# Cache pages loaded as 32 rows of 8 KB or as 128 rows of 2 KB, in a one-core decoder step

## The chip, the cores and the metric

The kernel runs on one core of a Trainium2 chip. The metric is the device time of one execution in microseconds (us). Its work is done by TensorE (matrix products), VectorE, ScalarE and GpSimd, and by 16 DMA engines that move data between DRAM and the on-chip memory of 128 partitions (SBUF). DMA instructions are issued by SyncE and GpSimd. In the profile TensorE is PE, VectorE DVE, ScalarE ACT, GpSimd POOL and SyncE SP.

## What is computed

One layer of a hybrid decoder for a prompt of 1024 tokens and for eight sample sequences of eight new tokens each. The part that the change touches is the attention of the samples over their cached past: 4096 tokens for each sequence, kept in pages of 128 tokens that a page table names. A token's row has 512 floats of keys (4 heads of 2 x 64) and 512 of values (4 heads of 128), 2 KB each.

```python
k_past = cache_k[i, page_table].reshape(DB, past_len, DIFF_HEADS, 2, DIFF_DH)
v_past = cache_v[i, page_table].reshape(DB, past_len, DIFF_HEADS, DIFF_DV)
...
s_past = jnp.einsum('bqhcd,bkhcd->bhcqk', q, k_past).astype(F32) * scale
a = jax.nn.softmax(jnp.concatenate([s_past, s_new], axis=-1), axis=-1)
w = (a[:, :, 0] - lam * a[:, :, 1]).astype(v.dtype)
return (jnp.einsum('bhqk,bkhv->bqhv', w[..., :P], v_past)
        + jnp.einsum('bhqk,bkhv->bqhv', w[..., P:], v))
```

All old tokens are visible to all new ones. With 8 sequences of 32 pages, 256 pages of keys and 256 of values are read, 256 KB each, 134 MB in all.

## The kernel before

The program runs its phases one after the other: input projection, gated linear attention, `attention`, and the dense stages (output projection, FFN, embedding). The phase `attention` interleaves two jobs. One is the causal attention of the prompt, in 32 units (4 heads by 8 query blocks). The other is the paged attention of the samples, in 64 groups of four pages (`NKV`), eight for each sequence.

TensorE, ScalarE and VectorE each follow an order written out by hand over `STEPS` = 74 steps. In step t, for t below 64, TensorE turns the keys of group t: four transposes of 128 x 128 for each of the four heads (line 1587), reading `m.kr[:, slot, p, ...]`, where p is the page in the group. ScalarE and VectorE copy them to `dec_kt`, and a step later the scores are formed (L1599). Nine steps behind (`LAG`), in step t, the group t - 9 has its exponentials transposed (L1622) and multiplied with its values (L1641), reading `m.vr[:, slot, p, ...]`. Transposes and products of the prompt lie in between (L1560, L1569, L1547). So steps 0 to 8 have keys alone, steps 9 to 63 keys and values, and steps 64 to 73 values alone.

`m.kr` (keys, tile `dec_k`) and `m.vr` (values, tile `dec_v`) are rings of four slots, of four pages each (`KR`, `VR` = 4): a slot is 128 partitions by 4 x 512 floats. `load_pages` (L1299) fills a slot with four DMAs, one for each page; the page number is read from the table into a register first. SyncE issues the key groups, in the gated-linear-attention phase the first three (`PRE`), and group n, from 4 on, after TensorE has turned the last head of group n - 4 (semaphore `ring_filled`, L1390). On its queue lie also the loads of the prompt's keys (L1309, 64 partitions each, lower and upper half in turn) and queries (L1316). GpSimd issues the value groups: the first four when TensorE has turned key groups 0, 2, 4 and 6, and group n when the values of group n - 4 have been used (`pv_done`, L1422). TensorE waits for the four DMAs of a group in `turn_keys` (L1581) and `values` (L1638).

Other transfers that are looked at below: the prompt and sample activations `x_in` at the start (L289: 128 partitions in rows of 4 KB; L294: 64 partitions), followed by weights in rows of 512 B, and `feat_swap` (L316), a copy inside SBUF from 32 partitions to 32 others in rows of 4368 B.

Of the kernel before, what the change touches and what calls it, by code (L numbers as in the profile page):

```python
# [829 lines left out]
def gla(nc, io, m, ps, scr, sems):  # L830
# [31 lines left out]
    with nc.Block() as block:  # L862

        @block.sync
        def _(sp):

            sp.dma_start(m.gvs[:, :], scr["gv_s"]).then_inc(s["v_loaded"], 16)
            sp.dma_start(m.gv[:, NC // 2:NC, :], scr["gv_p"].rearrange("(c p) f -> p c f", p=P)[:, NC // 2:NC]
                         ).then_inc(s["v_loaded"], 16)
            for pr in range(2):  # L870
                sp.dma_start(m.s0[:, pr], io["state_gla"][0, :, 2 * pr:2 * pr + 2].rearrange("b h k v -> (h k) b v")
                             ).then_inc(s["s_loaded"], 16)
            sp.wait_ge(table_in, 16)
            load_pages(sp, m.ids, io["cache_k"], m.kr, 0, pages_in[0], 0)
            for part in range(4):
                load_keys(sp, m, scr, 0, part, head_k_in)
            for n in range(2):
                load_queries(sp, m, scr, n, head_q_in[n])
            for n in range(1, PRE):
                load_pages(sp, m.ids, io["cache_k"], m.kr, n, pages_in[n], n)  # L880
            sp.wait_ge(s["kd_turned"], NC)
            sp.wait_ge(s["q1_ready"], 2 * NC)
            sp.wait_ge(s["qpe_ready"], 2)
            sp.wait_ge(s["s_kd"], 1)
            sp.dma_start(m.qs[:, :, :], scr["qS"].rearrange("h p t -> p h t")).then_inc(new_in, 16)
            sp.dma_start(m.kts[:, :, :], scr["kS"].rearrange("h p t -> p h t")).then_inc(new_in, 16)
            sp.dma_start(m.table[:, :], io["page_table"].rearrange("(o b) n -> o (b n)", o=1)).then_inc(ids_in, 16)
            sp.dma_start(m.lam[:, :, :], io["lam_params"].broadcast_to([P, 4, DK])).then_inc(lam_in, 16)
            sp.wait_ge(s["s_updated"], 2 * NC)
            for pr in range(2):  # L890
                sp.dma_start(io["new_gla_prompt"][2 * pr:2 * pr + 2].rearrange("h k v -> (h k) v"), m.s[:, pr]
                             ).then_inc(s["stored"], 16)
# [406 lines left out]
def load_pages(eng, ids, cache, ring, slot, sem, n):  # L1299

    for p in range(4):
        page = eng.value_load(ids[0:1, 4 * n + p:4 * n + p + 1], min_val=0, max_val=POOL - 1)
        eng.dma_start(ring[:, slot, p:p + 1, :], cache[bass.ds(page, 1)].rearrange("o t f -> t o f")).then_inc(sem, 16)  # L1303


def load_keys(eng, m, scr, h, part, sem):
# [12 lines left out]
def attention(nc, io, m, ps, scr, sems):  # L1319
# [57 lines left out]
    with nc.Block() as block:  # L1377

        @block.sync
        def _(sp):  # L1380
            sp.wait_ge(ids_in, 16)
            for n in range(PRE, KR):
                load_pages(sp, m.table, io["cache_k"], m.kr, n, k_page_in[n], n)
# [1763 lines left out]
```

## Time and profile before

| | |
|---|---|
| three runs, us | 1882.27, 1882.73, 1886.83 |
| median, us | 1882.73 |
| span of the profiled execution, us | 1880.3 |
| attention phase within the span | about 433 to 868 us |
| TensorE busy over the whole span | 1773.0 us (94%) |
| VectorE, ScalarE, GpSimd busy | 1192.5 (63%), 735.6 (39%), 341.2 us (18%) |
| bytes moved by DMA | 265.73 MB, mean 141 GB/s |

The profiled execution has a record of its span alone, from the first to the last instruction: 1880.3 us, 2.4 us below the median of the three runs. Times in rows are microseconds from the start of the span. A row with `x8` merges or groups eight instructions; `a<-b` means that tile a is written from tile b; L1587 is line 1587. The granted clock of TensorE (PEclk) is a share of full speed, and DMA share is the mean busy share of the 16 DMA engines; it can come out a little over 1.

### The profile page before, as it was taken

To read this page: it belongs to the slowest core of one execution; us is meant where nothing else is said; L and a number is where in the kernel's file an instruction comes from. 1 tells how busy PE (TensorE), PEld (TensorE's weight loads), DVE (VectorE), ACT (ScalarE), POOL (GpSimd) and SP (SyncE) were. 2 spreads that over 40 slices of the span, in tenths; PEclk is the share of its full clock that TensorE was granted. 3 is DMA by queue.
4 is the path that set the end of the run, shared out by engine and by line. 5 is a ranking of instruction groups with operands and counts; after the bars stand their busy time and mean duration, and the time that the engine had idled before them with its cause. 6 is when DMAs were issued, how large, how long until landed. Compare 5 with 4: busy or idle time off the path is not lost.

```text
span 1880.3 us, 35481 instructions
## 1 busy us (share of the span) xinstructions
PE 1773.0 (94%) x13062; PEld 1639.1 (87%) x13062; DVE 1192.5 (63%) x1946; ACT 735.6 (39%) x1418; POOL 341.2 (18%) x360
## 2 busy tenths in 40 slices
PE   6999999996999999996999999999999999999998
PEld 6999999984666667665998999999999999999997
DVE  4223742475777777765458876667677878699443
ACT  5113322564655565653225333222323424245320
POOL 1111331001233333332111211211121000000110
PEclk9999999898999999998999999999999999999998
DMA  5323551227999999977111222222222424232121
GB/s 162 108 80 82 141 140 56 61 83 236 330 350 354 346 357 360 353 231 226 35 45 46 80 69 81 81 70 69 81 70 69 157 81 134 74 106 86 47 69 48
DMA packets 232923, 265.73 MB, mean 141 GB/s; under 512 B 16162, under 2 KB 173428, under 8 KB 232756
## 3 DMA queue, kind: packets, MB, share of 16 engines
q1 hardware_dynamic: 211988, 195.36, 33.2%
q0 software_dynamic: 20768, 68.17, 10.7%
q8 instruction: 101, 1.65, 0.4%
q14 instruction: 66, 0.54, 0.1%
HBM read 229.79 MB, written 29.21 MB: 138 GB/s over the span
## 4 chain that ended last, share of the span: by engine, by line
PE 45%; DVE 6%; ACT 1%; issue 1%; DMA 1%; POOL 0%; DVEq 0%; ACTq 0%
PE psum L2518 33%; PE psum L150 10%; DVE x_second_lo L2532 1%; DVE unit_lo L1910 1%; DMA x_first_hi_raw<-scratch_z 1%; PE psum L2197 0%; PE psum L2894 0%; DVE x_second_lo_raw L2536 0%; DVE rstd_and_products L2576 0%; DVE x_first_lo L2532 0%; DVE h L2576 0%; ACT unit_hi L1904 0%; DVE rstd_and_products L2009 0%; DVE x_lo L2226 0%; DMA w_raw<-in_w_ple_gate 0%
## 5 line engine op out<-in xcount | busy, mean ns | idle before, releaser
L2518 PE MATMUL psum<-x_second_hi,unit_hi 128*128 128x364 f32 x924 | 304.5, 330 | 8.0 <-DVE x_second_lo L2532 4.6
L2518 PE MATMUL psum<-x_second_hi,unit_lo 128*128 128x364 f32 x924 | 303.4, 328 | 0.0
L2518 PE MATMUL psum<-x_second_lo,unit_hi 128*128 128x364 f32 x924 | 303.4, 328 | 0.0
L1303 POOL DMA_DIRECT2D dec_v<-in_cache_v x256 | 137.6, 538 | 288.1 <-issue 282.2
L150 PE MATMUL psum<-x_hi,w_hi 128*128 128x364 f32 x768 | 182.0, 345 | 5.8 <-DVE x_lo L2226 5.8
L2518 PEld LDWEIGHTS psum<-x_second_hi,unit_hi 128*128 128x128 f32 x924 | 173.8, 188 | 10.8 <-issue 5.7
L2518 PE MATMUL psum<-x_first_hi,unit_hi 128*128 128x364 f32 x528 | 173.7, 329 | 0.6 <-DVE x_first_lo L2532 0.6
L2518 PEld LDWEIGHTS psum<-x_second_hi,unit_lo 128*128 128x128 f32 x924 | 174.0, 188 | 0.0
L2518 PEld LDWEIGHTS psum<-x_second_lo,unit_hi 128*128 128x128 f32 x924 | 173.7, 188 | 0.0
L2518 PE MATMUL psum<-x_first_hi,unit_lo 128*128 128x364 f32 x528 | 173.5, 329 | 0.0
L2518 PE MATMUL psum<-x_first_lo,unit_hi 128*128 128x364 f32 x528 | 173.2, 328 | 0.0
L150 PE MATMUL psum<-x_hi,w_lo 128*128 128x364 f32 x768 | 170.2, 330 | 0.0
L150 PE MATMUL psum<-x_lo,w_hi 128*128 128x364 f32 x768 | 169.8, 329 | 0.0
L1470 ACT ACTIVATE dec_kt<-psum 128x512 f32<-128x512 f32 x192 | 108.6, 599 | 154.6 <-PE psum L1587 154.6
L1904 ACT ACTIVATE unit_hi<-unit_sums 128x512 fp32r<-128x512 f32 (+1 forms) x136 | 83.3, 618 | 217.2 <-PE psum L2518 184.7
L1587 PE MATMUL psum<-consts,dec_k 128*128 128x128 f32 x1024 | 139.3, 281 | 20.2 <-DMA dec_k<-in_cache_k 8.8
L2397 POOL TENSOR_TENSOR w_raw<-w_raw,gains 128x1024 f32<-128x1024 f32 x42 | 88.7, 2111 | 379.6 <-DMA w_raw<-in_w_ffn_gate 210.8
L1904 ACT ACTIVATE unit_hi<-w_raw 128x512 fp32r<-128x512 f32 (+1 forms) x136 | 82.5, 617 | 178.2 <-PE psum L2518 155.8
L1587 PEld LDWEIGHTS psum<-consts,dec_k 128*128 128x128 f32 x1024 | 115.2, 143 | 39.2 <-issue 15.7
L150 PEld LDWEIGHTS psum<-x_hi,w_hi 128*128 128x128 f32 x768 | 131.5, 189 | 15.2 <-DVE x_lo L2226 6.2
L150 PEld LDWEIGHTS psum<-x_lo,w_hi 128*128 128x128 f32 x768 | 133.9, 189 | 0.0
L150 PEld LDWEIGHTS psum<-x_hi,w_lo 128*128 128x128 f32 x768 | 133.8, 189 | 0.0
(313 smaller groups left out, 3313.3 us busy)
## 6 DMA issues: line engine op xcount, KB each, us to landing
dec_k<-in_cache_k SPq DMA_DIRECT2D x256, 256.0 KB, 5.7
dec_v<-in_cache_v POOLq DMA_DIRECT2D x256, 256.0 KB, 5.5
w_raw<-in_w_in SPq DMA_DIRECT2D x25, 512.0 KB, 3.9
scratch_z<-ffn_hidden SPq DMA_DIRECT2D x22, 546.0 KB, 2.8
w_raw<-in_w_ffn_gate SPq DMA_DIRECT2D x22, 512.0 KB, 3.8
w_raw<-in_w_ffn_up SPq DMA_DIRECT2D x22, 512.0 KB, 3.8
w_raw<-in_w_ffn_down SPq DMA_DIRECT2D x16, 512.0 KB, 4.0
feat_swap<-feat_n SPq DMA_DIRECT2D x32, 136.5 KB, 2.4
```

What stands on the lines that cost most here:

```text
L150: ins = pe.matmul(out[:, c, 0:SPAN], w(k), x(k)[:, c * SPAN:c * SPAN + SPAN], start=n == 0 and w is whi and x is xhi, stop=n == len(ks) - ...
L1303: eng.dma_start(ring[:, slot, p:p + 1, :], cache[bass.ds(page, 1)].rearrange("o t f -> t o f")).then_inc(sem, 16)
L1470: act.activation(m.kt[:, t % 2, h, :], ring_bank(("keys", t, h)), ACT.Copy).then_inc(d["ring_act"], 1)
L1587: ins = pe.transpose(ring_bank(key)[:, p * P:p * P + P], m.kr[:, t % KR, p, h * P:h * P + P], ident)
L1904: act.activation(m.uhi[unit][:, 0:half_tiles(t), :], unit_source(m, t, unit), ACT.Copy).then_inc(s["w_hi"], 1)
L1910: dve.tensor_tensor(m.ulo[unit][:, 0:n, :], unit_source(m, t, unit), f32(m.uhi[unit][:, 0:n, :]), ALU.subtract).then_inc(s["w_lo"], 1)
L2397: gp.tensor_tensor(m.raw[:, u], m.raw[:, u], gain(m, "ffn").unsqueeze(2).broadcast_to([P, KT, P]), ALU.mult).then_inc(s["w_scaled"], 1)
L2518: ins = pe.matmul(bank[b], w[unit][:, j, :], x[slot][:, j, :], start=start and j == 0 and w is m.uhi and x is m.xhi7, stop=j == k - 1 and ...
L2532: dve.tensor_tensor(m.xlo7[slot][:, 0:n, :], source, f32(m.xhi7[slot][:, 0:n, :]), ALU.subtract).then_inc(s["x_lo"], 1)
```

## The change

Each of the four DMAs of a group still moves one page of 256 KB to the same slot. Before, the page's 128 tokens went to 128 partitions, 2 KB each, in column block p of the slot. After, the page goes to 32 partitions, 32p to 32p+31: partition 32p + t receives the four neighbouring tokens 4t to 4t+3, side by side in the four column blocks, one row of 8 KB in DRAM and in SBUF. A column block of the slot then holds 32 tokens of each of the four pages. The change applies to keys and values alike.

```diff
     for p in range(4):
         page = eng.value_load(ids[0:1, 4 * n + p:4 * n + p + 1], min_val=0, max_val=POOL - 1)
-        eng.dma_start(ring[:, slot, p:p + 1, :], cache[bass.ds(page, 1)].rearrange("o t f -> t o f")).then_inc(sem, 16)
+        eng.dma_start(ring[32 * p:32 * p + 32, slot, :, :].rearrange("t j f -> t (j f)"),
+                      cache[bass.ds(page, 1)].rearrange("o (t j) f -> (o t) (j f)", j=4)).then_inc(sem, 16)
```

## Rows read from the trace of the kernel before

**Rows 1.** Busy time by stretch: us and (instructions) of each engine, clock, DMA share, GB/s.

```profile
core 0: us, PE busy (x) PEld busy (x) DVE busy (x) ACT busy (x) POOL busy (x), PEclk, DMA share, GB/s
433.00:494.00 61.00, 45.12 (x333) 30.46 (x337) 37.52 (x83) 29.16 (x70) 10.55 (x18) 0.88 0.98 316
494.00:828.00 334.00, 314.95 (x3937) 234.94 (x3927) 247.96 (x523) 200.51 (x513) 114.63 (x214) 1.00 1.00 342
828.00:868.00 40.00, 27.11 (x422) 19.15 (x420) 19.41 (x38) 12.37 (x37) 18.29 (x29) 0.86 0.69 211
500.00:800.00 300.00, 281.31 (x3510) 209.10 (x3502) 223.10 (x473) 180.11 (x462) 102.94 (x192) 1.00 1.02 352
```

**Rows 2.** TensorE's waits from 425 to 870 us: total us, times, longest us.

```profile
PE psum L1587 <- DMA dec_k<-in_cache_k: 8.8, 1, 8.8
...
PE psum L1641 <- DMA dec_v<-in_cache_v: 4.5, 2, 2.4
```

**Rows 3.** Waits of SyncE, which issues the key loads, from 433 to 868 us.

```profile
SPq L1302 <- PE psum L1587: 51.1, 30, 4.2
```

**Rows 4.** TensorE in order of time: start us, us, line, what it writes and reads.

```profile
494.05 1.06 PE L1641 MATMUL psum<-dec_v,dec_pt 128*32 128x128 f32 x32
...
826.73 1.04 PE L1587 MATMUL psum<-consts,dec_k 128*128 128x128 f32 x8
...
830.30 1.06 PE L1641 MATMUL psum<-dec_v,dec_pt 128*32 128x128 f32 x32
```

**Rows 5.** DMA queues from 500 to 800 us: packets, MB, share of 16 engines.

```profile
q1 hardware_dynamic: 32183, 54.64, 53.0%
q0 software_dynamic: 15349, 50.29, 48.3%
```

**Rows 6.** DMA from 3 to 14 us: all packets, then the queue of SyncE.

```profile
DMA packets 1297, 4.53 MB, mean 412 GB/s; under 512 B 208, under 2 KB 208, under 8 KB 1297
...
q1 hardware_dynamic: 1297, 4.53, 102.8%
```

**Rows 7.** DMA from 157 to 162 us; last line: issues, KB each, us to landing.

```profile
DMA packets 192, 0.56 MB, mean 112 GB/s; under 512 B 64, under 2 KB 64, under 8 KB 192
...
q1 hardware_dynamic: 192, 0.56, 50.3%
...
feat_swap<-feat_n SPq DMA_DIRECT2D x4, 136.5 KB, 2.4
```

**Rows 8.** DMA from 377.0 to 378.6 us, the same columns.

```profile
DMA packets 260, 0.44 MB, mean 278 GB/s; under 512 B 43, under 2 KB 43, under 8 KB 260
...
q1 hardware_dynamic: 260, 0.44, 84.7%
...
att_k<-scratch_kT SPq DMA_DIRECT2D x2, 128.0 KB, 3.2
```

**Rows 9.** DMA from 14.7 to 15.7 us, and from 16.2 to 17.6 us.

```profile
DMA packets 204, 0.19 MB, mean 186 GB/s; under 512 B 15, under 2 KB 179, under 8 KB 204
...
DMA packets 807, 0.41 MB, mean 290 GB/s; under 512 B 15, under 2 KB 807, under 8 KB 807
```

**Rows 10.** SyncE's queue in order of time, one merged piece of eight key loads.

```profile
606.12 8.86 SPq L1303 DMA_DIRECT2D dec_k<-in_cache_k  x8
```

**Rows 11.** DMA of the opening stretch (433 to 494 us), and issues from 828 us.

```profile
DMA packets 9625, 19.25 MB, mean 316 GB/s; under 512 B 1192, under 2 KB 1892, under 8 KB 9618
...
dec_v<-in_cache_v POOLq DMA_DIRECT2D x27, 256.0 KB, 3.7
```

**Rows 12.** Issuing a DMA on SyncE: duration ns min/median/max, first and last start.

```profile
L1303 SPq DMA_DIRECT2D dec_k<-in_cache_k x256: 332/338/3964, 368.2 to 809.3; - x128
...
L316 SPq DMA_DIRECT2D feat_swap<-feat_n x32: 507/591/606, 157.0 to 260.4; - x32
```

**Rows 13.** Busy time by stretch, ahead of the phase; columns as in rows 1.

```profile
420.00:440.00 20.00, 14.39 (x135) 12.22 (x133) 12.43 (x30) 10.33 (x35) 1.97 (x2) 0.83 0.28 92
```


## The prediction

> **What bounds the kernel now.** I first asked for the busy times of the engines in four stretches, because the change only touches the attention phase, which lies between 433 and 868 us [rows 1]. In the long middle stretch TensorE is busy 315 of 334 us at full granted clock, so at first sight it sets the pace. The column to look at beside it is the DMA share: 1.00, and 1.02 between 500 and 800 us. The 16 DMA engines are occupied all the time as well, and move 342 to 352 GB/s. Two resources are full at once, and the next question is who waits for whom.
>
> TensorE's own waits over the phase [rows 2] name a DMA in two rows only: 8.8 us once for a key page and 4.5 us in two pieces for value pages. The list of the DMA-issuing queue [rows 3] shows the reverse: SyncE waits 51 us in 30 pieces for TensorE to empty a slot of the key ring. So the loads run ahead of TensorE, by up to the four groups that each ring holds, and are throttled by it. TensorE bounds the phase and the DMA engines just keep up: anything that lowers their rate by more than a few per cent makes them the bound.
>
> The rhythm follows from TensorE's order of instructions [rows 4]. The value products of step 9 (the first ones) begin at 494.05 us, those of step 63 (the last step that also turns keys) at 830.30 us. That is 54 steps in 336.3 us, 6.23 us each. In each the DMA engines move 342 GB/s x 334 us / 53.6 steps = 2.13 MB: one group of four key pages, one of four value pages, and a few queries. The break-even rate is therefore 2.13 MB / 6.23 us = 342 GB/s.
>
> **The change part by part.** The number of DMA instructions (256 for keys, 256 for values), their bytes, their semaphores and their places in the queues stay the same. What changes is the shape: 32 rows of 8 KB to 32 partitions, where 128 rows of 2 KB went to 128. Inside a group, token 4t+j of a page now sits at partition t, block j, for keys and values alike. A softmax sum doesn't depend on the order of its terms and all old tokens are visible, so no instruction is added on any compute engine: 0 us there.
>
> *Packets.* Today 192 value loads leave 15349 packets on their queue [rows 5]: 192 x (64 + 16) = 15360, so two rows already share a packet of 4 KB, plus 16 completion packets. Larger packets help where the DMA is the bound. 4 KB rows to 128 partitions move 4.53 MB in 102.8% of 11 us, 400 GB/s of busy time [rows 6], against 345 GB/s (352 / 1.02) for the present mix. Were the destination as wide as now, the DMA would gain some slack, and TensorE would only lose its two DMA waits: at most 13 us.
>
> By the Trainium skill, DMA: Bandwidth & Descriptors, "Why small descriptors are slow", a packet costs about three fixed cycles beside one for every 32 bytes. An estimate from that page is 67 cycles for 2 KB and 259 for 8 KB, 3% less per byte; it speaks for the change, and no run here isolates it.
>
> *Destination.* What speaks against the change is the width. The trace has one transfer of the new width: `feat_swap`, four DMAs of 136.5 KB, each to 32 partitions in rows of 4368 B [rows 7]. They leave 64 small completion packets, 16 for each, so all 16 DMA engines take part. But 0.56 MB occupies them for 50.3% of 5 us: 222 GB/s, or 13.9 GB/s for an engine where the wide load got 25. It isn't a perfect twin (SBUF to SBUF), so I looked for loads from DRAM. The keys of the prompt go to 64 partitions, the upper and the lower half in turn, in rows of 2 KB [rows 8]: 0.44 MB in 84.7% of 1.6 us, 325 GB/s. At 14.7 us, where the 64-partition `x_in` sample is mixed with the weights queued behind it, the rate falls to 0.19 MB in 1 us, 186 GB/s, between 400 GB/s before [rows 6] and 290 GB/s after it, with the weights alone in rows of 512 B [rows 9]. I read these as: narrow transfers to the same half of the partitions slow each other to about half, those to different halves little.
>
> The Trainium skill states a reason in SBUF — State Buffer, "Door 1: The DMA port swizzle": partitions 0 to 31 reach 8 of 16 ports, with 218 GB/s as the asymptote and 189 GB/s at 1 MiB, and two loads to partitions 0 and 64 at once gained 6%. The 222 GB/s of [rows 7] agree with its asymptote, the 325 GB/s of [rows 8] with its 6% do not. By that page alone the whole phase would go at about 200 GB/s, which is an estimate; the rival below works such a case out from rows.
>
> In a group, pages 0 and 1 go to the lower half of the partitions and pages 2 and 3 to the upper. The key group is issued by SyncE after the step's transposes, the value group by GpSimd after the value products, and SyncE often issues two groups on end [rows 10]. Nothing ties a key page to a value page on the same half, so I take half of the bytes at 222 GB/s (same half) and half at 325 GB/s (other half): (4.50 + 3.08) / 2 = 3.79 us per MB, 264 GB/s. The bounds are 186 GB/s below [rows 9] and 400 GB/s above [rows 6]; I stay nearest to [rows 7], the only row of the same width.
>
> *The sum.* A step takes 2.13 x 3.79 = 8.07 us in place of 6.23: 54 x 1.84 = 99 us. The opening, 433 to 494 us, moves 19.25 MB [rows 11]: 73 us in place of 61, 12 us. In the tail, 828 to 868 us, only values are left: 27 value loads (7.1 MB) at 222 GB/s take 32 of its 40 us [rows 1, 11], so little is lost there: 2 us. Together 113 us. The span of 1880.3 us becomes 1993 us; the three runs have their median 2.4 us above that span, so the forecast is 1996 us.
>
> *Costs taken as nothing.* SyncE needs 338 ns to issue a key load and 591 ns for a 32-partition `feat_swap` [rows 7, 12]. Four times 0.25 us is 1 us a step on a queue that waited about 1 us a step for TensorE [rows 3]; uncovered it would be a few us in all, and in a step of 8.07 us it is covered. GpSimd's issue lies on an engine with nothing else to do. TensorE's 315 us in 334 become about 5.9 us of work in a step of 8.07 us, 73% busy; where it was busy 72% (14.39 of 20 us) its granted clock was 0.83 on average, between its two levels of 1.2 and 2.4 GHz [rows 13]. At 0.83 the 5.9 us become 7.1 us and stay hidden behind the DMA. At the lower level throughout they would not, but then TensorE would again be busy all the time.
>
> **The rivals.** *Half rate throughout* (chance 0.28). The DMA engines work through key and value pages in step, so that they meet on the same half whichever page is up. For it: [rows 7, 9]. Against it: [rows 8]. At 222 GB/s a step takes 9.60 us, 54 x 3.37 = 182 us, the opening 26 us more, the tail 3: 211 us, 2094 us. At the 186 GB/s of [rows 9] it is 282 + 42 + 6 = 330 us, 2213 us.
>
> *No difference* (0.11). Key and value pages lie on different halves most of the time, or the slow `feat_swap` belongs to SBUF as a source and not to the destination; then the rate stays at or over the 342 GB/s of the break-even and TensorE goes on setting the step. For it: the 325 GB/s of [rows 8] are close to it already. The change would also do nothing if 8 KB rows were cut into packets of today's size and the width didn't matter. 1883 us.
>
> *Faster* (0.11). As before, but the larger rows lift the rate towards the 400 GB/s of [rows 6] and the key wait of 8.8 us at the opening and the value waits of 4.5 us in the tail go away: 1883 - 13 = 1870 us. It decides itself at a sustained rate over 342 GB/s in the middle stretch; under that it can't be.
>
> **How the numbers follow.** The forecast, a phase bound by the DMA with halves partly shared, has 0.50 (some 1890 to 2060 us). Two runs of this kernel differ by up to 0.3%, which is about what can be told from no change. The first two cases are slower: 0.78; no difference 0.11; faster 0.11. The range reaches from 1878 us, which takes in the case of no difference, to 2150 us, which takes in the half-rate case down to about 205 GB/s; left out are the faster case and some 0.07 above.
>
> **What would show it right or wrong.** Right: in the changed profile the value products of steps 9 and 63 lie about 436 us apart, DMA share stays near 1.00 while the rate drops to about 264 GB/s, TensorE waits some 100 us for key or value pages inside the middle stretch, SyncE's waits for TensorE remain but the loads land later, and value loads leave 32 + 16 packets each. The granted clock in the middle stretch falls under 1.00. The time after the phase is unchanged. Wrong: a rate of 342 GB/s or more at the new width (the width doesn't bind), or about 222 or less with the step at 9.6 us (no sharing of halves at all), or TensorE's work itself longer.

## The result and the profile after

The changed kernel takes 2053.25 us (median; 2046.95 to 2057.34), the one before 1884.78 us in the same runs. The ratio is 1.0893, with a 95% interval from 1.0874 to 1.0912: some 168 us slower. The span of the profiled execution grew from 1880.3 to 2051.7 us, by 171.4 us.

Nearly all of it lies in the attention phase, which now reaches to about 1040 us (868 before); what follows takes 1012 us in both. The busy times by stretch answer to [rows 1] (us and instructions of each engine, granted clock, DMA share, GB/s):

```profile
core 0: us, PE busy (x) PEld busy (x) DVE busy (x) ACT busy (x) POOL busy (x), PEclk, DMA share, GB/s
433.00:494.00 61.00, 37.96 (x245) 26.13 (x245) 27.89 (x65) 21.05 (x49) 9.87 (x18) 0.79 1.00 238
494.00:1000.00 506.00, 368.00 (x4065) 280.90 (x4059) 262.00 (x549) 213.59 (x538) 105.71 (x216) 0.89 1.01 236
1000.00:1040.00 40.00, 23.57 (x388) 16.85 (x379) 17.73 (x34) 10.40 (x31) 16.49 (x26) 0.86 0.84 193
```

The two columns that were both full before have come apart. The DMA share of the middle stretch is still 1.01, but 236 GB/s pass where 342 did. TensorE is busy 368 of 506 us instead of 315 of 334: 6.6 us in a step instead of 5.9. The granted clock has fallen from 1.00 to 0.89 of full speed, in the same proportion, and the rest of the stretch is waiting. In the tail, with values alone, 193 GB/s pass (211 before).

The waits show who waits for whom now: first TensorE's two waits for a DMA, as in [rows 2], then SyncE's for TensorE, as in [rows 3] (total us, times, longest us), and last the time of a key load from issue to landing:

```profile
PE psum L1588 <- DMA dec_k<-in_cache_k: 140.9, 40, 14.4
PE psum L1642 <- DMA dec_v<-in_cache_v: 11.0, 4, 3.7
...
SPq L1302 <- PE psum L1588: 215.6, 48, 10.5
...
DMA to landing us min/median/max: 3.3/24.0/36.7
```

TensorE's 8.8 us for key pages have become 140.9 us in 40 pieces. SyncE still waits for TensorE, even longer than before (216 us against 51): it issues a group as soon as a slot is empty, and then a load of the group is under way for 24.0 us in the median, where it was 5.7 us before. So neither the issue nor the ring is late; the transfer itself is slow.

TensorE in order of time gives the step, as in [rows 4]: the value products of step 9, the last keys of step 63, and its value products.

```profile
509.97 1.06 PE L1642 MATMUL psum<-dec_v,dec_pt 128*32 128x128 f32 x32
...
995.67 1.04 PE L1588 MATMUL psum<-consts,dec_k 128*128 128x128 f32 x8
...
999.23 1.06 PE L1642 MATMUL psum<-dec_v,dec_pt 128*32 128x128 f32 x32
```

54 steps in 489.3 us are 9.06 us each, against 6.23. That is 153 of the 171 us. The opening ends 15.9 us later (first value products at 509.97 instead of 494.05 us), and 2.5 us are left for the tail and all that follows.

The DMA queues from 500 to 800 us answer to [rows 5]: all packets, then each queue with packets, MB and share of the 16 engines.

```profile
DMA packets 15787, 71.50 MB, mean 238 GB/s; under 512 B 4800, under 2 KB 6968, under 8 KB 7480
...
q1 hardware_dynamic: 9786, 38.42, 55.3%
q0 software_dynamic: 5961, 32.59, 46.5%
```

From such a row follows how fast one DMA engine moves a queue's bytes while it is at work on them. The value queue has 32.59 MB in 46.5% of 16 x 300 us, 14.6 GB/s for an engine, and the key queue 14.5 GB/s. In [rows 5] the same sum gives 21.7 and 21.5 GB/s. The time of a packet includes any time for which it is held up. This "rate per engine" is used for all kernels below.

### The profile page after: what moved, and what is told of

Its sections match the earlier page's. It is cut to its first block and busy times, and to the rows that moved or that the text cites. A ratio compares the mean times of both kernels' runs of the same rounds, so it can differ in the third digit from the quotient of the medians.

```text
span 2051.7 us, 35481 instructions
## 1 busy us (share of the span) xinstructions
PE 1814.5 (88%) x13062; PEld 1678.9 (82%) x13062; DVE 1193.6 (58%) x1946; ACT 738.9 (36%) x1418; POOL 332.3 (16%) x360
## 5 line engine op out<-in xcount | busy, mean ns | idle before, releaser
L1588 PE MATMUL psum<-consts,dec_k 128*128 128x128 f32 x1024 | 168.7, 319 | 147.0 <-DMA dec_k<-in_cache_k 140.9
L1588 PEld LDWEIGHTS psum<-consts,dec_k 128*128 128x128 f32 x1024 | 141.4, 166 | 167.4 <-DMA dec_k<-in_cache_k 155.9
L1303 POOL DMA_DIRECT2D dec_v<-in_cache_v x256 | 125.3, 490 | 471.6 <-issue 465.7
L1752 DVE COPY dec_kt<-psum 128x512 f32<-128x512 f32 x64 | 44.2, 691 | 245.6 <-PE psum L1588 245.6
```

The lines of the kernel that those rows point to most:

```text
L1303: eng.dma_start(ring[32 * p:32 * p + 32, slot, :, :].rearrange("t j f -> t (j f)"), cache[bass.ds(page, 1)].rearrange("o (t j) f -> (o t) ...
L1588: ins = pe.transpose(ring_bank(key)[:, p * P:p * P + P], m.kr[:, t % KR, p, h * P:h * P + P], ident)
L1752: dve.tensor_copy(m.kt[:, t % 2, h, :], ring_bank(("keys", t, h))).then_inc(d["ring_dve"], 1)
```

## The experiments

Two theories stood at the start. A: the destination is narrow, and DMA engines that write to the same part of the partitions hold each other up. B: rows of 8 KB are slow in themselves. All diffs are against the changed kernel and abridged: where one has plus lines alone, the lines that they replace are left out, and comments in it are explanations. The windows of busy times and queues are 520 to 820 us, in the columns of the first fence.

**stride4: the same rows, spread over all partitions.**

```diff
-        eng.dma_start(ring[32 * p:32 * p + 32, slot, :, :].rearrange("t j f -> t (j f)"),
+        eng.dma_start(ring[p::4, slot, :, :].rearrange("t j f -> t (j f)"),
```

> Each page still goes out as 32 rows of 8 KB, but to the partitions p, p+4, p+8, ..., 124+p, so every single DMA reaches over all 128 partitions. Theory A (the narrow destination is slow: the DMA engines that write to the same 32 neighbouring partitions hold each other up): the middle stretch goes back to the rate that TensorE asks for, about 342 GB/s and 6.2 us a step, 1870 to 1900 us. Theory B (rows of 8 KB are slow in themselves, wherever they go): as the changed kernel, 9.06 us a step at 238 GB/s, about 2053 us. In between, some 1950 us, if engines still meet in pairs on the same part of the memory.

Measured: 1887.83 us, ratio to the kernel before 1.0016 [1.0004, 1.0029]. The busy times of the window, and below them the two queues:

```profile
520.00:820.00 300.00, 281.29 (x3513) 208.99 (x3506) 222.94 (x472) 180.19 (x461) 99.29 (x192) 1.00 0.98 353
...
q1 hardware_dynamic: 13595, 54.68, 49.0%
q0 software_dynamic: 9264, 50.61, 47.7%
```

353 GB/s, 23.2 and 22.1 GB/s per engine, and a step of 6.23 us. The rows, the packets and the number of DMAs are those of the changed kernel; only the 32 partitions are other ones. That removes the whole loss but 3 us, so B falls as a cause of it. The rate of 353 GB/s is what TensorE asks for; what these rows could do beyond it, the run doesn't show.

**rows2k: the same partitions, small rows.**

```diff
-        eng.dma_start(ring[32 * p:32 * p + 32, slot, :, :].rearrange("t j f -> t (j f)"),
-                      cache[bass.ds(page, 1)].rearrange("o (t j) f -> (o t) (j f)", j=4)).then_inc(sem, 16)
+        eng.dma_start(ring[32 * p:32 * p + 32, slot, :, :],
+                      cache[bass.ds(page, 1)].rearrange("o (j t) f -> t (o j) f", j=4)).then_inc(sem, 16)
```

> Each page goes to the same 32 partitions as in the changed kernel, but as 128 separate rows of 2 KB (tokens t, 32+t, 64+t, 96+t on partition t), so destination width is that of the changed kernel and row size that of the kernel before. Theory A (destination): still about 2053 us, 9.06 us a step, within 40 us. Theory B (row size): back to about 1885 us.

Measured: 2056.0 us, ratio 1.0889 [1.0855, 1.0923], as slow as the changed kernel.

```profile
520.00:820.00 300.00, 218.58 (x2352) 168.24 (x2351) 150.65 (x320) 123.28 (x310) 70.81 (x129) 0.87 1.05 236
...
q1 hardware_dynamic: 21003, 35.67, 54.5%
q0 software_dynamic: 10553, 34.59, 50.2%
```

The packet counts show that the rows are small again: value packets carry 3.3 KB on average, as in [rows 5], and key packets 1.7 KB. The rate is 236 GB/s all the same, 13.6 and 14.4 GB/s per engine. With stride4 this settles it from both sides: the partitions decide, and the row size makes a difference of 1% in the rate and none in the time that could be seen. What it is inside the destination that the DMA engines share, neither run shows.

**wide64 and stride2_half: which partitions belong together?** wide64 sends 64 rows of 4 KB to a whole half of the partitions; stride2_half sends 32 rows of 8 KB to every second partition of a half.

```diff
+        at, b = 64 * (p // 2), 2 * (p % 2)
+        eng.dma_start(ring[at:at + 64, slot, b:b + 2, :].rearrange("t j f -> t (j f)"),
+                      cache[bass.ds(page, 1)].rearrange("o (t j) f -> (o t) (j f)", j=2)).then_inc(sem, 16)
```

```diff
+        at = 64 * (p // 2)
+        eng.dma_start(ring[at + p % 2:at + 64:2, slot, :, :].rearrange("t j f -> t (j f)"),
+                      cache[bass.ds(page, 1)].rearrange("o (t j) f -> (o t) (j f)", j=4)).then_inc(sem, 16)
```

> Each page goes as 64 rows of 4 KB (two tokens) to 64 neighbouring partitions, pages 0 and 1 to the lower half, pages 2 and 3 to the upper. Theory A in the form that halves of the partitions matter: no gain over 32 partitions, about 2053 us, within 30. Theory A in the form that the number of partitions matters, and theory B (row size): about half the way back, 1930 to 1990 us.

> Each page goes as 32 rows of 8 KB to every second partition of one half: pages 0 and 1 to the even and odd partitions of 0 to 63, pages 2 and 3 to those of 64 to 127. If what counts is the half of the partitions that a transfer reaches, this is as slow as 64 neighbouring partitions: 236 to 255 GB/s in the middle stretch, 2020 to 2055 us. If what counts is that the 32 partitions of the changed kernel are neighbours, this goes back to the kernel before, as the spacing of four over all 128 partitions did: about 1887 us.

Measured: wide64 2030.91 us, ratio 1.0767 [1.0714, 1.082]; stride2_half 2047.33 us, ratio 1.0869 [1.0846, 1.0892]. The window of wide64, then that of stride2_half with its queues:

```profile
520.00:820.00 300.00, 223.34 (x2483) 168.84 (x2482) 159.39 (x336) 130.12 (x329) 72.07 (x140) 0.89 1.04 250
```

```profile
520.00:820.00 300.00, 216.58 (x2416) 164.51 (x2414) 154.03 (x324) 125.91 (x320) 67.46 (x135) 0.89 1.02 240
...
q1 hardware_dynamic: 9333, 36.64, 52.5%
q0 software_dynamic: 6371, 34.80, 49.3%
```

Twice as many partitions raise the rate only from 238 to 250 GB/s, and gaps between the partitions do nothing as long as they stay in one half (240 GB/s). What stride4 has and these two don't is a reach over both halves in each DMA. (wide64 also has rows of 4 KB, a change to which rows2k gives no weight.)

The Trainium skill, SBUF — State Buffer, "Door 1: The DMA port swizzle", has 189 GB/s for 32 partitions and 196 for 64, 4% more, because both reach the same 8 of 16 ports. The step of 5% from 238 to 250 GB/s agrees with it; the level here is above the 218 GB/s that it gives as the limit of 8 ports. Loads to both halves are in the queues here, which may be the reason; no run shows it.

**alt_halves and values_turned: does it matter which pages meet?** alt_halves only changes the order of the four places, so that neighbours in a queue lie on different halves. values_turned moves the values of page p to the place of page p + 2.

```diff
+        at = (0, 64, 32, 96)[p]
+        eng.dma_start(ring[at:at + 32, slot, :, :].rearrange("t j f -> t (j f)"),
```

```diff
+        q = (p + turn) % 4          # turn is 2 for the values, 0 for the keys
+        eng.dma_start(ring[32 * q:32 * q + 32, slot, :, :].rearrange("t j f -> t (j f)"),
```

> As the changed kernel, but the four pages of a group go to partitions 0, 64, 32, 96 in this order, so that neighbours in the queue lie on different halves. If two transfers to different halves run beside each other as the forecast assumed (325 GB/s against 222 on the same half), engines that are a page ahead no longer meet the others: a step of 6.6 to 8 us, 1905 to 1995 us. If the engines run through the pages in step, each page is as slow as before and the order doesn't matter: 2053 us within 15.

> As the changed kernel, with the values of page p on the partitions that page p + 2 had, so that the halves of key and value pages are exchanged against each other (the weights meet the values of other tokens; the work is the same). The forecast took key and value pages to meet on the same half for half of their bytes, without order. If so, turning one of them changes nothing: 2053 us within 12. If they meet with a fixed offset in the changed kernel, the rate moves by more than that, to either side: towards 222 GB/s (up to 2095 us) or towards 264 GB/s (down to 2000 us).

Measured: alt_halves 2026.87 us, ratio 1.0757 [1.0727, 1.0786]; values_turned 2049.61 us, ratio 1.0901 [1.0857, 1.0946]. The two windows:

```profile
520.00:820.00 300.00, 229.19 (x2541) 172.98 (x2540) 163.93 (x345) 131.65 (x335) 70.00 (x143) 0.88 1.02 254
```

```profile
520.00:820.00 300.00, 218.88 (x2413) 166.59 (x2412) 155.34 (x327) 125.75 (x317) 66.41 (x135) 0.88 1.02 239
```

Exchanging the halves of key and value pages changes nothing (239 GB/s). Either they don't meet in a fixed order in the changed kernel, as the forecast had assumed, or it makes no difference where they meet. Alternating the halves within the queues lifts the rate to 254 GB/s and shortens the step from 9.06 to 8.47 us, in an execution that was 11 us faster than the median. That is a gain, but a small one, and 2026.87 us lie outside what I expected of either case: neighbours in a queue gain little from lying on different halves. Which pages are under way at the same time, no run shows.

**keys_only and values_only: half of the change.** One of the two caches has the new shape, the other is loaded over 128 partitions as before.

```diff
-                load_pages(gp, m.table, io["cache_v"], m.vr, n % VR, v_page_in[n % VR], n)
+                load_pages(gp, m.table, io["cache_v"], m.vr, n % VR, v_page_in[n % VR], n, False)   # False: in the old form
```

> Only the key pages have the new shape; values are loaded as before, over 128 partitions (the weights meet the values of other tokens; the work is the same). If every byte of a narrow load costs the DMA engines 1/238 us per KB and a wide one 1/345, as the two kernels have it, a step takes 2.13 x (0.5/0.238 + 0.5/0.345) = 7.56 us, 72 us over the kernel before: about 1957 us, 1940 to 1980. If wide loads beside them are held up to the same extent (engines wait for the narrow packets of others), it comes near the changed kernel, 2010 us or more; if wide loads fill the gaps, nearer to 1885, under 1930 us.

> Only the value pages have the new shape; keys are loaded as before (the weights meet the values of other tokens; the work is the same). As for the keys alone: by the sum 1957 us (1940 to 1980), 2010 or more if the wide loads are held up too, under 1930 if they fill the gaps. A difference between this run and the one with narrow keys would belong to the queue (SyncE's or GpSimd's) and not to the width.

Measured: keys_only 2024.24 us, ratio 1.0751 [1.0733, 1.0769]; values_only 2014.34 us, ratio 1.0712 [1.0683, 1.0742]. Half of the change costs some 80% of the whole. The queues of keys_only (keys on q1, narrow; values on q0, wide) with one of TensorE's waits over the phase (425 to 1060 us), then the same of values_only (values on q0, narrow):

```profile
q1 hardware_dynamic: 9810, 38.51, 54.9%
q0 software_dynamic: 10588, 34.72, 47.4%
...
PE psum L1646 <- DMA dec_v<-in_cache_v: 102.1, 35, 6.8
```

```profile
q0 software_dynamic: 6824, 37.28, 53.9%
q1 hardware_dynamic: 22464, 38.24, 48.9%
...
PE psum L1592 <- DMA dec_k<-in_cache_k: 107.6, 23, 14.1
```

The narrow queue moves 14.6 and 14.4 GB/s per engine, as in the changed kernel. The wide queue beside it no longer moves 21.7 or 21.5 but 15.3 and 16.3 GB/s: it is held up as well. That is the case of "2010 us or more" in the expectation, for both queues alike, so it doesn't belong to SyncE's or GpSimd's way of issuing; the 10 us between the two runs are within their intervals. In keys_only TensorE waits longest for the wide values, not for the narrow keys; in values_only it waits for the keys, as in the changed kernel. A plausible reason is that a wide load has rows for the half that the narrow pages fill just then, and isn't complete before its last row; the runs show the slowing, not this reason.

**narrow16 and spread16: half as many rows in a DMA.** A page goes out in two DMAs of 16 rows, to 16 neighbouring partitions or to every eighth one. The waits for a group count eight DMAs instead of four.

```diff
+        rows = cache[bass.ds(page, 1)].rearrange("o (t j) f -> (o t) (j f)", j=4)
+        for a in (0, 16):
+            at = 32 * p + a                                 # spread16: at = p + a // 4
+            eng.dma_start(ring[at:at + 16, slot, :, :]        # spread16: ring[at::8, slot, :, :]
+                          .rearrange("t j f -> t (j f)"), rows[a:a + 16]).then_inc(sem, 16)
```

> Each page goes out in two DMAs of 16 rows of 8 KB, each to 16 neighbouring partitions (a quarter of a half); every DMA engine moves one row. If only the half of the partitions counts, nothing more is lost: 2053 us, up to 2100 with twice as many DMAs to issue. If the destination has more, smaller parts that are shared (so that 16 partitions reach half as many of them as 32 do), the rate falls again: by a full halving, 119 GB/s, a step would take 17.9 us and the kernel about 2530 us; with neighbours in the queue overlapping, 2100 to 2500 us.

> The control for the run above: also two DMAs of 16 rows of 8 KB for a page, but to every eighth partition, over all 128. It shows what twice as many DMAs cost by themselves. SyncE needs about 0.9 us for a load with its page number and some 0.5 us for the second half: 4 x 1.4 us and the queries are about 6.2 us a step, GpSimd 4 x 1.6 us about 6.5: 1885 to 1920 us if the destination is the only cause, and anything over that is the issue of the DMAs.

Measured, in one run each and so without an interval: narrow16 2184.78 us, spread16 2057.56 us. The queues of narrow16 and SyncE's wait for TensorE (425 to 1060 us), then the same of spread16, with the duration of its key issue (ns, min/median/max) and one merged piece of eight key loads:

```profile
q1 hardware_dynamic: 9591, 31.04, 54.1%
q0 software_dynamic: 6733, 27.65, 48.3%
...
SPq L1302 <- PE psum L1590: 184.4, 44, 8.9
```

```profile
q1 hardware_dynamic: 11946, 38.46, 49.0%
q0 software_dynamic: 8604, 35.22, 45.9%
...
L1306 SPq DMA_DIRECT2D dec_k<-in_cache_k x512: 495/503/3185, 368.3 to 977.7; - x171
...
SPq L1302 <- PE psum L1590: 0.9, 4, 0.3
...
602.79 7.49 SPq L1306 DMA_DIRECT2D dec_k<-in_cache_k  x8
```

narrow16 is slower again, at 12.0 and 11.9 GB/s per engine, while SyncE waits 184 us for TensorE, so that its issue isn't the bound: still narrower costs more, though far less than a second halving. spread16 failed as a control. SyncE almost never waits for TensorE in it (0.9 us), so its own issue, at 503 ns for the DMA alone, keeps the keys back: the eight loads of a group take it 7.5 us, and with the queries a step comes to about 9 us, where the expectation had 6.2. Its time can't be put down to the destination. Its rates per engine, 16.4 and 16.0 GB/s against 23.2 in stride4, hint that every eighth partition isn't a full reach either, although each of these DMAs reaches both halves; but it is one run of a kernel that its issue holds back as well.

## Why the prediction came out as it did

*The bound.* Right: TensorE set the pace and the DMA engines just kept up, so a lower rate turned the phase over to them. The DMA share stayed at 1.01 and the rate fell under the break-even of 342 GB/s.

*Packets.* Right in the count: a value load leaves 48 packets (5961 for 32.59 MB, which are 124 loads). That larger packets help where the DMA is the bound did not show: at the narrow width, rows of 2 KB and of 8 KB move at 236 and 238 GB/s. It had no price in the sum.

*Destination.* That the width of the destination makes the DMA engines the bound was right: stride4 takes the loss away with nothing changed but the partitions. The size was not. The forecast had half of the bytes at 222 GB/s and half at 325, 264 together; measured are 238. The narrow rate of 222 GB/s ([rows 7]) was nearly right. The step that failed is the 325 GB/s from [rows 8] for pages on different halves. In the runs nothing near it appears: alternating halves give 254 GB/s, exchanging them 239.

The row was also misread. SyncE issues a key page over all 128 partitions just ahead of the prompt's keys, on the same queue. Below are both issues in the kernel before (start us, us), the page's time from issue to landing, and the DMA from 377 to 382 us, up to the next key page:

```profile
375.18 0.34 SPq L1303 DMA_DIRECT2D dec_k<-in_cache_k  x1
375.56 0.52 SPq L1309 DMA_DIRECT2D att_k<-scratch_kT  x1
...
dec_k<-in_cache_k SPq DMA_DIRECT2D x1, 256.0 KB, 3.5
...
DMA packets 737, 0.95 MB, mean 190 GB/s; under 512 B 146, under 2 KB 402, under 8 KB 737
```

The page lands at 378.7 us, after the end of the window of [rows 8] (377.0 to 378.6 us). The prompt's keys and queries behind it, four loads of 128 KB and four of 64 KB, are 0.79 MB of the 0.95 MB; the other 0.16 MB belong to the page, and the window of [rows 8] holds 0.44 MB. So the 325 GB/s are the rate of a mixture, about a third of it wide, and not of narrow loads on different halves. What such loads would do alone stays open.

One stretch has no value load beside the keys: key groups loaded ahead of the phase, 382 to 392 us, first in the changed kernel, then in the one before.

```profile
DMA packets 378, 2.01 MB, mean 201 GB/s; under 512 B 130, under 2 KB 134, under 8 KB 134
...
q1 hardware_dynamic: 376, 1.99, 83.2%
...
q1 hardware_dynamic: 1130, 2.07, 69.3%
```

1.99 MB in 83.2% of 10 us are 239 GB/s of busy time, as much as the two queues together in the phase. It fits with nothing being won from the other queue, but it doesn't prove it: the queue isn't full here, and for the wide loads the same sum gives 299 GB/s, under the 345 of the phase.

*The sum.* With 238 GB/s in place of 264 the same sum gives 8.95 us a step, 54 x 2.72 = 147 us, an opening of 81 us (20 us more) and 2 us of tail: 169 us, where 171.4 us were measured. So the form of the sum held, and one term carried the error: 99 us for the steps, against 153.

*Taken as nothing.* SyncE's issue, feared to grow to 591 ns, stayed at 321 ns:

```profile
L1303 SPq DMA_DIRECT2D dec_k<-in_cache_k x256: 320/321/1980, 369.6 to 964.6; - x128
```

The granted clock fell to 0.89 in the middle stretch, and no cost of its own shows: TensorE's 6.6 us of work in a step (368 us in 506) fit into 9.06 us, with the DMA share at 1.01.

*Rivals.* The half-rate case (2094 us at 222 GB/s) lies 41 us above the result, the forecast 57 us below it: in number the rival was nearer, and the result lies 7 us inside the 1890 to 2060 us of the forecast's case. The reason that the rival gave, key and value pages in step on the same half, isn't borne out: values_turned exchanges the halves, and nothing changes. The forecast of about 100 us of waiting for pages inside the middle stretch became 122 us (494 to 1000 us), of 152 us in the phase. "No difference" and "faster" needed 342 GB/s at the new width, and the narrow loads never came near it.

By the Trainium skill, SBUF — State Buffer, "Can I just issue two DMAs to hit both halves?", two loads to the two halves at once gain 6% over a single one. alt_halves gains 7% in rate over the changed kernel (254 against 238). That isn't quite the same comparison, as the changed kernel has loads to both halves in its queues too, but here the page was a better guide than [rows 8], where 325 against 222 GB/s stood for a gain of 46%.

## What to carry to other kernels

Where DMA engines are busy all the time, look at which partitions one DMA reaches before making its rows longer: 32 rows of 8 KB to neighbouring partitions cost 31% of the rate, and the same rows to every fourth partition cost none that shows at the rate TensorE asks for. A narrow load also slows the wide ones beside it, so changing half of the loads saves little. And before a rate is taken from a short window as the price of a transfer, see which other transfers land in it, and how full the queue is.

## What was not expected of the hardware

The issue of a DMA on SyncE takes longer for some shapes of the destination: 338 ns for 128 partitions and 321 ns for 32 neighbours ([rows 12] and above), but 481 ns for every fourth partition in stride4, and then 477 ns in wide64:

```profile
L1303 SPq DMA_DIRECT2D dec_k<-in_cache_k x256: 480/481/2077, 368.9 to 811.7; - x128
...
L1304 SPq DMA_DIRECT2D dec_k<-in_cache_k x256: 477/477/3039, 368.7 to 944.0; - x128
```

The 64 partitions of wide64 are neighbours, so the spacing alone isn't the reason; it stays open. In stride4 the longer issue was hidden. With twice as many DMAs, in spread16, it was not.

A wide load beside narrow ones lost almost as much as they did, 15.3 to 16.3 GB/s per engine in place of 21.6; I had expected the two to add up, 1957 us instead of 2014 and 2024.
